# Convolving the V channels of a gated DeltaNet layer in token-major form, with row-shifted copies made by DMA

## The reference

```python
proj = h @ w_in                       # 2048 -> 4096 (q, k: 2048 each), 4096 (v), 4096 (z), 64 gates
qkv = jax.nn.silu(_causal_depthwise_conv(qkv, conv_w))     # 4 taps along the tokens, per channel
q, k, v = _split(qkv, [GDN_QK_W, GDN_QK_W, GDN_V_W])
...
o = _from_chunks(_gated_delta_chunkwise(q, k, v, log_alpha, beta))
o = _head_rmsnorm(o) * norm_w
```

## Time and profile before

| | us |
|---|---|
| median of 3 runs (lowest, highest) | 2721.97 (2721.55, 2723.23) |
| the profiled execution | 2722.66 |
| its span, first to last instruction | 2720.9 |
| TensorE busy | 2704.4 |
| VectorE busy | 1806.8 |
| ScalarE busy | 1411.5 |
| GpSimd busy | 93.7 |

### The profile page before, as it was taken

One profiled execution on the slowest core, in us unless ns is written; L12 is line 12 of the kernel. 1 busy time (PEld: TensorE's weight loads), 2 busy tenths in 40 slices (PEclk: granted clock), 3 DMA queues, 4 the chain that ended last, 5 costly groups with the idle time before them and its releaser, 6 DMA issues.

```text
span 2720.9 us, 37018 instructions
## 1 busy us (share of the span) xinstructions
PE 2704.4 (99%) x13170; PEld 2251.1 (83%) x13170; DVE 1806.8 (66%) x2538; ACT 1411.5 (52%) x2005; POOL 93.7 (3%) x80
## 2 busy tenths in 40 slices
PE   8999999999999999999999999999999999999998
PEld 7888888888888888888888888888888888888887
DVE  5544678666666666668797978656767666666444
ACT  5444555444444444458787778554454444444443
POOL 0000000000000000001111111000000000000000
PEclk9999999999999999999999999999999999999999
DMA  8564466666666656666564656555666666666664
GB/s 259 158 199 143 153 200 187 201 193 193 193 193 193 193 190 196 194 196 187 156 190 152 189 175 192 171 180 189 193 193 194 193 192 194 192 193 194 207 196 158
DMA packets 264736, 510.95 MB, mean 188 GB/s; under 512 B 20497, under 2 KB 21265, under 8 KB 264353
## 3 DMA queue, kind: packets, MB, share of 16 engines
q1 hardware_dynamic: 260064, 493.95, 59.5%
q0 software_dynamic: 3152, 11.57, 1.3%
q10 hardware_dynamic: 1392, 3.77, 0.4%
HBM read 503.95 MB, written 5.28 MB: 187 GB/s over the span
## 4 chain that ended last, share of the span: by engine, by line
PE 96%; DVE 3%; DMA 0%; ACT 0%; issue 0%; DVEq 0%; SPq 0%; ACTq 0%
PE acc L604 30%; PE acc L605 30%; PE acc L610 30%; PE aux L847 1%; DVE wlo L1545 1%; PE aux L691 1%; PE aux L859 1%; PE aux L852 1%; PE aux L841 0%; PE aux L833 0%; DVE const L1990 0%; DVE arena L1990 0%; DMA wraw<-in_l_w_in 0%; DVE arena L2031 0%; DVE arena L2028 0%
## 5 line engine op out<-in xcount | busy, mean ns | idle before, releaser
L1545 DVE TENSOR_TENSOR wlo<-wraw,whi 128x1024 fp32r<-128x1024 f32 x928 | 1137.0, 1233 | 708.0 <-ACT whi L1056 704.4
L1056 ACT ACTIVATE whi<-wraw 128x1024 fp32r<-128x1024 f32 x928 | 978.4, 1059 | 1101.9 <-PE acc L610 1062.5
L604 PE MATMUL acc<-whi,hT_hi 128*128 128x512 f32 x2624 | 1035.2, 395 | 1.8 <-DVE hT_lo L1737 1.2
L605 PE MATMUL acc<-whi,hT_lo 128*128 128x512 f32 x2624 | 1024.2, 390 | 0.0
L610 PE MATMUL acc<-wlo,hT_hi 128*128 128x512 f32 x2624 | 703.1, 390 | 0.5 <-DVE wlo L1545 0.5
L604 PEld LDWEIGHTS acc<-whi,hT_hi 128*128 128x128 f32 x2624 | 493.4, 188 | 104.0 <-DVE hT_lo L1737 1.5
L610 PEld LDWEIGHTS acc<-wlo,hT_hi 128*128 128x128 f32 x2624 | 492.2, 188 | 103.5 <-DVE wlo L1545 1.3
L605 PEld LDWEIGHTS acc<-whi,hT_lo 128*128 128x128 f32 x2624 | 494.0, 188 | 99.1
L604 PE MATMUL acc<-whi,arena 128*128 128x512 f32 x1072 | 417.7, 390 | 0.0
L605 PE MATMUL acc<-whi,arena 128*128 128x512 f32 x1072 | 417.6, 390 | 0.0
L610 PE MATMUL acc<-wlo,arena 128*128 128x512 f32 x1072 | 286.7, 390 | 0.0
(11 more groups left out here) (269 smaller groups left out, 1188.1 us busy)
## 6 DMA issues: line engine op xcount, KB each, us to landing
wraw<-in_l_w_in SPq DMA_DIRECT2D x304, 512.0 KB, 4.2
wraw<-in_l_w_gate SPq DMA_DIRECT2D x176, 512.0 KB, 3.6
wraw<-in_l_w_up SPq DMA_DIRECT2D x176, 512.0 KB, 3.6
wraw<-in_l_w_down SPq DMA_DIRECT2D x176, 512.0 KB, 4.3
wraw<-in_l_w_out SPq DMA_DIRECT2D x96, 512.0 KB, 4.6
arena<-decay_sums POOLq DMA_DIRECT2D x16, 512.0 KB, 5.3
o_rounds<-arena POOLq DMA_DIRECT2D x3, 1024.0 KB, 6.0
arena<-o_rounds ACTq DMA_DIRECT2D x3, 1024.0 KB, 5.3
```

The lines of the kernel that those rows point to most:

```text
L604: nc.tensor.matmul(pair[m], hi[:, k, tok], wh, start=first, stop=False)
L605: nc.tensor.matmul(pair[m], lo[:, k, tok], wh, start=False, stop=False)
L1056: nc.scalar.activation(whi[:, s, :], wraw[:, s, :], ACT.Copy).then_inc(hi_done, 1)
L1545: V.tensor_tensor(wlo[:, s, :], wraw[:, s, :], whi[:, s, :].bitcast(F32), ALU.subtract).then_inc(lo_done, 1)
```

## The change

V0 and V1 are no longer transposed. They stay token-major in `qkv`, and the shift by 1, 2 and 3 tokens, which crosses partitions, is made by DMA. Per block of 512 channels:

- ScalarE issues six DMAs in one slot (`lags`): for each lag of 1, 2 and 3, one from 128 - lag partitions of `qkv` to the partitions `lag` further down (two runs of 2 KB in each partition), and a small one that carries the last `lag` tokens of the first half to the first `lag` partitions of the second. V0's stand in slot -4 (in round 0 in slot -2), V1's in slot 15.
- VectorE multiplies the block and its three shifted copies by taps (4 products of 128 x 1024), zeroes three rows, and adds them up (3 sums of 128 x 1024): `v_conv`, in slots 5, 8 and 9 for V0 and 23, 24, 27 and 28 for V1. The first part waits for the six DMAs and for the taps.
- ScalarE applies silu in slots 11 and 30 and scales into `v_tok` in slots 13 and 31.
- GpSimd loads the taps, the same in all partitions (1 MB per block), from a new input array.

The shifted copies of lags 1 and 2 and the taps use the SBUF space of `x`: GpSimd stores `x` to DRAM (2 MB) when layer 0 is complete, and loads it back after the last convolution. Four groups of 8 transposes per round go away (`conv_transposes` and `token_major` of V0 and V1), with the two `tap`s and the two `conv`s of V. `load_o` and a few of the gating steps after the rounds are moved by some units. TensorE's wait for the previous round's last addition moves from slot 0 to slot 4, and its wait for the masked KQ product from slot 27 to slot 32.

```diff
+            def store_x():
+                pool.wait_ge(xs_copied, 8)
+                pool.dma_start(x_dram[:, :], xflat).then_inc(x_stored, 16)
+                pool.wait_ge(x_stored, 16)
...
+            def taps(r, b):
+                n, col = V_BLOCK(r, b), P * conv_tile(r, b)
+                if n:
+                    pool.wait_ge(v_sum, n)
+                pool.dma_start(tap_rows, A["conv_rows"][:, col:col + NB].rearrange("(a w) n -> a w n", a=1).to_broadcast([P, CW, NB])
+                               ).then_inc(taps_in, 16)
...
-                if s == 0:
-                    if r:
-                        pe.wait_ge(end_dve, END_DVE(r - 1, "o1"))
-                    conv_transposes(V0, aux[1])
...
-                if s == 10:
...
-                    token_major(V0, aux[0])
-                if s == 15:
-                    pe.wait_ge(tok_copy, TOK_AT(r, V0))
+                if s == 15:
+                    pe.wait_ge(tok_copy, TOK_AT(r, K))
                     conv_transposes(Q, aux[0])
...
-                if s == 27:
-                    pe.wait_ge(kq_mask, r + 1)
-                    conv_transposes(V1, aux[0])
...
-                if s == 31:
-                    pe.wait_ge(conv_sum, TOK_AT(r, V1))
-                    token_major(V1, aux[0])
...
+                def lags(b):
+                    n = V_BLOCK(r, b)
+                    act.wait_ge(acc_read[b % 2], (BLOCK0["l1"] + 4 * r + b) // 2 + 1)
...
+                    for lag in range(1, CW):
+                        dst = row_lag[lag - 1]
+                        act.dma_start(dst[lag:, :, :], qkv[0:P - lag, :, v_cols(b)]).then_inc(v_lags, 16)
+                        act.dma_start(dst[0:lag, 1, :], qkv[P - lag:, 0, v_cols(b)]).then_inc(v_lags, 16)
...
+                if s == (FIRST_SLOT if r else -2):
+                    lags(V0)
...
+                if s == 15:
+                    lags(V1)
...
+                if s == 11:
+                    v_rows_silu(V0)
...
+                def v_conv(b, part):
+                    n, v = V_BLOCK(r, b), qkv[:, :, v_cols(b)]
+                    tap = lambda lag: tap_rows[:, CW - 1 - lag, :].unsqueeze(1).to_broadcast([P, M, NB])
+                    if part == 0:
+                        dve.wait_ge(taps_in, 16 * (n + 1))
+                        dve.wait_ge(v_lags, 16 * V_LAGS * (n + 1))
...
+                        V.tensor_tensor(v, v, tap(0), ALU.mult)
+                        V.tensor_tensor(row_lag[0], row_lag[0], tap(1), ALU.mult).then_inc(v_step, 1)
+                    if part == 1:
+                        V.tensor_tensor(row_lag[1], row_lag[1], tap(2), ALU.mult)
+                        V.tensor_tensor(row_lag[2], row_lag[2], tap(3), ALU.mult).then_inc(v_step, 1)
+                    if part == 2:
...
+                        V.tensor_tensor(v, v, row_lag[0], ALU.add).then_inc(v_step, 1)
...
+                        V.memset(row_lag[2][0:CW - 1, 0, :], 0.0)
...
+                        V.tensor_tensor(v, v, row_lag[1], ALU.add).then_inc(v_step, 1)
+                    if part == 3:
...
+                        V.tensor_tensor(row_lag[2], v, row_lag[2], ALU.add).then_inc(v_sum, 1)
...
-                if s == 2:
-                    conv(V0)
+                if s == 5:
+                    v_conv(V0, 0)
...
+                if s == 8:
+                    v_conv(V0, 1)
+                if s == 9:
+                    v_conv(V0, 2)
+                    v_conv(V0, 3)
...
+                if s in (23, 24):
+                    v_conv(V1, s - 23)
...
-                if s == 27:
-                    conv(V1)
+                if s in (27, 28):
+                    v_conv(V1, s - 25)
```

More of the change, by code:

```diff
@@ L163 @@
 D_AT = counts(0, 1)
-TOK_AT = counts(K, V0, Q, V1)
-CONV_TR_AT = lambda r, b: b + 1 if r == 0 else 3 * r + 1 + b
+TOK_AT = counts(K, Q)
+CONV_TR_AT = lambda r, b: 1 if b == K else r + 2
+V_BLOCK = lambda r, b: 2 * r + (b == V1)
+V_STEPS, V_LAGS = 4, 2 * (CW - 1)
 GRAM_AT = counts("kk", "kq")
@@ L254, in build @@
         qkv = at(0, [P, M, 2048])
+        xflat = x[:, :, :].rearrange("p m n -> p (m n)")
         k_tok = at(16 * KB, [P, M, 512])
@@ L258, in build @@
         qkT = at(28 * KB, [P, 8, SEQ])
-        vT = C["decay"].rearrange("p (t n) -> p t n", n=SEQ)
+        row_lag = [xflat[:, 2 * NB * l:2 * NB * (l + 1)].rearrange("p (m n) -> p m n", m=M) for l in range(2)]
+        row_lag.append(C["decay"].rearrange("p (m n) -> p m n", m=M))
+        tap_rows = xflat[:, 4 * NB:8 * NB].rearrange("p (w n) -> p w n", w=CW)
         k_turned = at(36 * KB, [P, 4, SEQ])
@@ L300, in build @@
         aux = [ctx.enter_context(nc.psum_tensor(f"aux{i}", [P, 2 * NB], F32)) for i in range(2)]
-        conv_in = lambda r, b: flat(k_turned) if b == K and r else (aux[0], aux[1], aux[0], aux[0])[b]
+        conv_in = lambda r, b: flat(k_turned) if b == K and r else aux[0]
         aux4 = [aux[i // 2][:, (i % 2) * NB:(i % 2 + 1) * NB] for i in range(4)]
@@ L348, in build @@
         conv_silu = sem("conv_silu")
+        x_stored = sem("x_stored")
+        x_back = sem("x_back")
+        lag_zero = sem("lag_zero")
+        taps_in = sem("taps_in")
+        v_lags = sem("v_lags")
+        v_step = sem("v_step")
+        v_sum = sem("v_sum")
+        v_silu = sem("v_silu")
+        v_rows = sem("v_rows")
         tok_tr = sem("tok_tr")
@@ L558, in gdn @@
                 nc.gpsimd.memset(T[:], 0.0)
+                taps(r, V1)
                 if r == ROUNDS - 1:
@@ L576, in gdn @@
                     pool.wait_ge(lev_psum, LEVEL_PSUM(r, "TT64_1"))
+                    taps(r + 1, V0)
                     decay_rows(r + 1)
@@ L584, in _ @@
             keep_x("dn0")
+            store_x()
+            taps(0, V0)
             pool.wait_ge(gate_step, GATE_AT["sums_exp"])
@@ L591, in _ @@
                 gdn(r)
+            load_x()
             keep_x("out1")
@@ L1353, in value_rows @@
                             n = HV * c + 4 * (b == V1) + h
-                            a = nc.scalar.activation(v_tok[int(b == V1)][:, c, h, :], aux[0][:, c * NB + h * P:c * NB + (h + 1) * P], ACT.Copy,
-                                                     scale=small(3, n, 1))
-                    a.then_inc(tok_copy, 1)
+                            a = nc.scalar.activation(v_tok[int(b == V1)][:, c, h, :], row_lag[2][:, c, head(h)], ACT.Copy, scale=small(3, n, 1))
+                    a.then_inc(v_rows, 1)
                 def level_copy(step, dst, rows, cols):
@@ L1383, in gdn @@
                     nc.scalar.activation(small(2, 8, 8), small(2, 0, 8), ACT.Sqrt, bias=epsc[:, 0:1], scale=1.0).then_inc(root_set, 1)
-                if s == 7:
-                    silu(V0)
+                if s == 11:
+                    v_rows_silu(V0)
+                    if r == ROUNDS - 1:
+                        load_o(0)
                 if s == 9:
@@ L1414, in gdn @@
                     nc.scalar.activation(small(2, 32, 8), small(2, 24, 8), ACT.Sqrt, bias=epsc[:, 1:2], scale=float(GD)).then_inc(root_set, 1)
-                if s == 28:
-                    tap(V1)
-                if s == 28 and r == ROUNDS - 1:
+                if s == 30:
+                    v_rows_silu(V1)
+                if s == 30 and r == ROUNDS - 1:
                     load_o(1)
@@ L1424, in gdn @@
                 if s == 31:
-                    silu(V1)
-                if s == 32:
                     act.wait_ge(et_set, r + 1)
@@ L1463, in qkv_out @@
                     act.wait_ge(k_turns, r - 1)
+                elif r and q in (V0, V1):
+                    act.wait_ge(v_sum, V_BLOCK(r - 1, q) + 1)
                 elif r:
@@ L1497, in hook_l1 @@
                     qkv_out(b - 1)
-                if j == (5 if b in (Z_BLOCK + 2, Z_BLOCK + 3, Z_BLOCK + 4) else 3) and b > Z_BLOCK:
+                if j == {Z_BLOCK + 2: 5, Z_BLOCK + 3: 5, Z_BLOCK + 4: 7}.get(b, 3) and b > Z_BLOCK:
                     z_out(b - Z_BLOCK - 1)
@@ L1587, in add @@
                     dve.wait_ge(xhi_done, n + 4 * norm)
+                    if norm == 3 and isinstance(n, int) and n == 0:
+                        dve.wait_ge(x_back, 16)
                     V.tensor_tensor(xs[:], acc[parity][:, :, :], x[:, :, bass.ds(n * NB, NB)], ALU.add
```

38 lines of the change are left out of this document (29 added, 9 removed).

## The result

| | us |
|---|---|
| after, median of 6 runs (lowest, highest) | 2918.97 (2916.95, 2920.87) |
| before, 6 runs beside them | 2722.48 (2721.55, 2723.23) |
| ratio, 95% interval | 1.0721 (1.0709, 1.0732) |
| the profiled execution after, and its span | 2920.87, 2919.1 |

196.5 us slower; 2919 was predicted.

A forecast was written before the change was run, and what follows sets the result against it. TensorE was taken as the bound, busy 2704.4 of 2720.9 us. Sum: 2722.66 - 14.9 (transposes) + 22 (VectorE) + 187 (hold) + 2 (store) = 2918.8, about 2919 us; own range 2855 to 2955, wider range 2727 to 2950.

The forecast's parts named there:

- The transposes: On TensorE, 16 groups of 8 transposes of V at 0.93 us go away, saving 14.9 us.
- The dealing: How lag rows spread over 16 DMA engines: equal shares only, so 127 rows on 1, 126 on 14, 125 on 5.
- the 325 packets and 28.6 us: Load per block on the first DMA engine under equal shares; an even spread gives 48 packets and 4.2 us.
- The hold: ScalarE stuck in its second and last lag issues, 30 us per set; TensorE stalls 4 x (24.3 + 22.5) = 187 us.
- VectorE: Surplus V work stalls TensorE 6.2 us in each of rounds 1 to 3, 3.5 in round 0: together 22 us.
- at nothing: V1's extra VectorE work, 8.7 less 4.75 us in slots 22 to 30, beside TensorE's long groups, costed zero.
- The rest: Storing x in the layer's first units costs 2 us (0 to 5); load back, taps and moved waits add nothing.
- some 30 units to land: Time allowed for loading x back after the last convolution, so no cost was counted.
- The even spread: Rival: lag rows spread over all engines, only VectorE's 22 us and the store remain; 2732 us, chance 0.17.
- the faster one: Rival: even spread and VectorE's surplus of slots 5 to 20 swallowed; 2708 us, chance 0.08.
- One engine, no hold: Rival: ScalarE goes on, VectorE waits in slots 5 and 23 for the first DMA engine; 2795 us, chance 0.14.
- the ends 23 and 34: Shortest and longest hold of ScalarE, in us, used for the main forecast's own range, 2855 to 2955.

The follow-up runs named there:

- e1_split: The changed kernel with each big lag transfer (127, 126, 125 rows) cut into 112 rows and a rest, nine issues per block: 2780.12 us, ratio 1.0211.
- e9_spread: Against e1_split, the nine lag issues of a set spread over three slots, three of one lag in each: 2765.88 us, ratio 1.0160.
- e2_lag1_split: The changed kernel with only the 127-row lag 1 transfer cut, into 112 and 15 rows: 2777.0 us, single run.
- e3_pool_issues: The changed kernel with the six lag transfers in the same shapes, issued by GpSimd instead of ScalarE: 2894.35 us, single run.
- e12_v1_later: Against a 2736.72 us version (copies split and spread, x moved, V0 earlier, far products on GpSimd): V1's lag-1 product there too, first part slot 27; 2741.95 us.
- e8_pool_products: Against e1_split, the lag 2 and 3 products of each V block moved from VectorE to GpSimd: 2768.57 us, ratio 1.0166.

## Why the prediction was right, point by point

- **The transposes.** 16 groups of 0.93 us, 14.9: right. The unit with a group is 0.80 us shorter and the next one 0.13.
- **The dealing.** Equal shares, 127 rows on one engine: right as far as the counts of packets of 4 B, the DMA share of 0.07 and what cutting one transfer did can show it; the kernel before had transfers of 128 rows only on that queue, so its trace left the choice open. That all six transfers of a set begin on the same engine (the 325 packets and 28.6 us of the sum) is shown by no run; what the trace has is that a set's last row of 2 KB was moved 29 to 37 us after the start of its first.
- **The hold.** Its place (second issue of each set, and a short one at the sixth) is as written. That the queue takes nothing new until most of a transfer's packets are gone remains a reading; the second issue was let go at 128 to 154 of 254 rows. Its size was wrong: 187 us predicted, 163 measured. The sets took 24 to 30 us (30 assumed), with a second issue of 15.7 to 22.6; TensorE's stalls were 18.3 to 23.3 each and not 22.5 and 24.3. A packet of 2 KB took 84 ns, 88 were assumed, and the last issue was let go some 10 us before the last row was moved, where I had left 2 to 3. The lower clock behind each hold, some 1.5 us by my estimate from the 5.30 us for 3.62, was not in the sum; it is in the 163. With e1_split and e9_spread the issues are worth 139 and 14, 153 us.
- **VectorE.** 22 us predicted, 21 measured, most of it in slots 12 to 15 as argued. That they agree so well is luck: by round they were 5.3, 4.1, 3.4 and 8.5 and not 3.5 and three times 6.2, and the sums and products took 9.6 us for 8.7 (V1's first addition is the 2.92 us above). What failed is that I costed V1 "at nothing": V1's late sum holds GpSimd's queue, and with it two megabytes.
- **The rest.** This is the step that failed: the first units lost 9 us and not "2 us (0 to 5)", and the store isn't all of it, since the taps alone cost 6.1 there. "The taps (1 MB each) are asked for at least 13 units ahead", at no cost, missed that it matters when they pass, not only when they are needed; so did "some 30 units to land" for the load of `x`, some 6 us in round 3. Slot 33 cost 21. Together 2 predicted, 29 measured: almost exactly what the hold was over-sized by.
- **The rivals.** The even spread (2732) and the faster one (2708) needed all 16 engines. With at least 13 of them on each big copy, by the packet counts, e1_split still stood at 2780, 48 above that rival's sum, mostly by the same missed terms (slot 33, units 7 and 8) and 14 us of issues that I had costed at nothing. "One engine, no hold" at 2795 was not reproduced.
- **The sums.** With 187 us at a hold of 30, the ends 23 and 34 with VectorE's 10 and 34 give 2851 and 2963 and not 2855 to 2955; and the faster rival's 2708 leaves out the 2 us of the store. Neither changes a conclusion.

## What to carry to other kernels

Try a DMA of 127 rows on such a queue in two, of 112 and 15 (the issue behind it took 15.7 to 22.6 us whole, and 0.62 to 1.09 us in e1_split), and never let an engine on which TensorE waits issue anything behind the whole one: cutting one kind of transfer, eight of them, brought back some 140 us here. When an engine gets more work, follow its lateness into the queues that wait for its results: V1's late sum cost 14 us through loads that it delayed by 2 us. Count all side loads at the place where they pass. And a change that trades 15 us of TensorE for transfers, issues and VectorE work on other full engines has to pay for each; the best of the versions tried was still 0.5% behind.

## What the hardware showed that was not expected

- An issue of ScalarE behind the 127-row transfer takes 15.7 to 22.6 us (the kernel after), with the 16 engines busy for 18% in the stretch shown; it is let go when 128 to 154 of the 254 rows are moved. Behind the 126- and 125-row transfers of e2_lag1_split it takes 0.65 to 1.32 us.
- At each of the eight holds the granted clock falls to 0.50 of full speed, for 17 to 24 us, and in the one shown the first TensorE work behind it is slow: 5.30 us for what takes 3.62.
- The same copies issued by GpSimd (e3_pool_issues) become 21760 more packets, 17584 in all of 8 B, and their last small one lands after 40.7 us.
- VectorE's two-input subtraction takes up to 3.4 us instead of 1.22 while GpSimd multiplies (e12_v1_later), and in e8_pool_products moving 19.5 us of products to GpSimd took only 9.4 us off VectorE's busy time.
